# Moving the gating unit's layer norm, the query tiles and the first pair's set-up to other places of a one-core hybrid layer

## The reference, cut to what matters

```python
proj = xn @ p['w_in']
rw, gu, gv, q, gt = jnp.split(proj, [N_SHIFT, N_SHIFT + W, N_SHIFT + 2 * W, N_SHIFT + 3 * W], axis=-1)
rw_s = rw + p['mu_shift'] * (prev - rw)          # prev: the row of the token before
a_out, wkv_new = rwkv7_mix(rw_s, ...)            # 16 heads, matrix state, token recurrence
b_out, v_rows = sgu_mix(gu, gv, ...)             # gelu(gu) * (w_s @ layernorm(gelu(gv)) + b_s)
c_out = mem_xattn(q, mem_k, mem_v)               # 4 heads of 256 over 256 memory rows
gates = jax.nn.sigmoid(gt.reshape(B, T, N_BRANCH, D_MODEL))
mix = jnp.sum(gates * br, axis=2) @ p['w_out']   # br: the three outputs times w_branch
...
y = h + rmsnorm(f, p['g_post_ffn'])              # f: the channel mixer with its convolution
```

## Time and profile before

| | |
|---|---|
| median of 3 runs | 2741.54 us (2741.31 to 2742.99) |
| the profiled execution | 2740.34 us, of which the span from first to last instruction is 2738.4 us |
| PE busy | 2474.8 us, 90% of the span |
| DVE, ACT, POOL busy | 1532.1, 862.1, 98.6 us |
| granted TensorE clock, mean | 0.954 of 2.4 GHz |
| DMA | 346.73 MB, 127 GB/s on average |

### The profile page before, as it was taken

The page is one execution under the profiler, slowest core; times in us unless marked ns, Lnnn a source line. Parts: engine busy times, 40 slices in busy tenths (PEclk is TensorE's granted clock), DMA queues, the critical chain, the costliest instruction groups (busy, mean ns, idle before and its releaser), DMA issues.

```text
span 2738.4 us, 50132 instructions
## 1 busy us (share of the span) xinstructions
PE 2474.8 (90%) x19707; PEld 2321.2 (85%) x19707; DVE 1532.1 (56%) x2207; ACT 862.1 (31%) x940; POOL 98.6 (4%) x171
## 2 busy tenths in 40 slices
PE   5999998996899988988989898699999999999975
PEld 4799977895778777877789897699999999999975
DVE  4533443455556654665554435766566666666665
ACT  4343323422212221222133333333333333323323
POOL 2000000001000000000000000000000000000001
PEclk9999979997999999999999998799999999999987
DMA  5544327632223223322254433144444444444431
GB/s 183 192 145 146 123 92 247 242 108 61 71 78 89 78 89 96 89 73 70 82 155 145 153 124 121 62 154 139 153 138 154 153 143 148 141 155 148 150 126 51
DMA packets 280241, 346.73 MB, mean 127 GB/s; under 512 B 6735, under 2 KB 240511, under 8 KB 278381
## 3 DMA queue, kind: packets, MB, share of 16 engines
q1 hardware_dynamic: 270365, 308.44, 35.2%
q0 software_dynamic: 9712, 36.30, 4.1%
q10 hardware_dynamic: 32, 0.01, 0.0%
HBM read 333.83 MB, written 10.89 MB: 126 GB/s over the span
## 4 chain that ended last, share of the span: by engine, by line
PE 70%; DVE 15%; ACT 6%; issue 6%; DMA 2%; DVEq 1%; POOL 1%; ACTq 0%; SPq 0%; POOLq 0%
PE bank L225 21%; PE bank L227 19%; PE bank L226 19%; PE bank L1030 6%; ACT hi L209 3%; DVE lo L216 3%; DVE rw L1885 2%; DVE work L788 1%; DVE q L712 1%; DMA work<-in_cache_mem_k 1%; PE bank L427 1%; DVE rw L1883 1%; DMA raw<-in_w_branch 1%; PE bank L1450 1%; ACT rw L1827 1%
## 5 line engine op out<-in xcount | busy, mean ns | idle before, releaser
L225 PE MATMUL bank<-ah,hi 128*128 128x320 f32 x3232 | 1040.7, 322 | 50.4 <-DVE lo L216 27.1
L226 PE MATMUL bank<-al,hi 128*128 128x320 f32 x3232 | 1009.4, 312 | 0.0
L227 PE MATMUL bank<-ah,lo 128*128 128x320 f32 x3232 | 1009.4, 312 | 0.0
L216 DVE TENSOR_TENSOR lo<-raw,hi 128x2048 fp32r<-128x2048 f32 x286 | 655.7, 2293 | 626.7 <-ACT hi L209 612.9
L209 ACT ACTIVATE hi<-raw 128x2048 fp32r<-128x2048 f32 x286 | 547.7, 1915 | 1220.1 <-PE bank L227 1183.3
L225 PEld LDWEIGHTS bank<-ah,hi 128*128 128x128 f32 x3232 | 616.7, 191 | 79.4 <-issue 54.7
L226 PEld LDWEIGHTS bank<-al,hi 128*128 128x128 f32 x3232 | 617.9, 191 | 1.8 <-issue 0.4
L227 PEld LDWEIGHTS bank<-ah,lo 128*128 128x128 f32 x3232 | 616.7, 191 | 0.0
L225 PE MATMUL bank<-bh,hi 128*128 128x320 f32 x1088 | 346.2, 318 | 19.1 <-DVE bl L1900 18.3
L226 PE MATMUL bank<-bl,hi 128*128 128x320 f32 x1088 | 336.7, 309 | 0.0
L227 PE MATMUL bank<-bh,lo 128*128 128x320 f32 x1088 | 336.6, 309 | 0.0
(11 more groups left out here) (332 smaller groups left out, 1762.6 us busy)
## 6 DMA issues: line engine op xcount, KB each, us to landing
raw<-in_w_in SPq DMA_DIRECT2D x98, 1024.0 KB, 5.3
raw<-in_w_up SPq DMA_DIRECT2D x88, 1024.0 KB, 5.1
raw<-in_w_down SPq DMA_DIRECT2D x44, 1024.0 KB, 5.0
raw<-in_w_branch SPq DMA_DIRECT2D x24, 1024.0 KB, 5.7
raw<-in_w_out SPq DMA_DIRECT2D x16, 1024.0 KB, 5.4
raw<-in_w_mem_k SPq DMA_DIRECT2D x8, 1024.0 KB, 5.3
raw<-in_w_mem_v SPq DMA_DIRECT2D x8, 1024.0 KB, 5.0
work<-in_cache_mem_k POOLq DMA_DIRECT2D x8, 1024.0 KB, 5.7
```

The lines of the kernel that those rows point to most:

```text
L216: dve.tensor_tensor(lo[c % NS][:, :], raw[c % 2][:, :], hi[c % NS][:, :], ALU.subtract)\
L225: pe.matmul(out, a_hi, b_hi, start=first, stop=False)
L226: pe.matmul(out, a_hi, b_lo, start=False, stop=False)
L227: return pe.matmul(out, a_lo, b_hi, start=False, stop=last)
```

## The change

- The first units are now 16 (`guv_*`): first gv, then gu. The mean of v, its subtraction, the squares and their sum are made inside this stage, beside gu's units. The matmul of the mean stands between the loops over units.
- q's 8 units move behind it. `Beside` gives out 34 units: q's 8, then the rwkv tiles in the order `RW_ORDER` (the tiles of the low-rank inputs first). There are 66 steps before sc0's own (kt0 has 14 of them), 11 per sample as before, 48 in the prompt's pieces, 2 before `wz` and 3 before `wq` (two places in the first pair's set-up), and 65 after.
- In the gating unit the spatial weights are turned before v; four of the gates have 3 steps ahead of them instead of 1.
- ACT evicts an rwkv tile with three instructions instead of two; the samples' first tokens get their old state from one DVE instruction for all tiles.
- Attention's output is split per head of 256 (`split_heads_*`), three of the four inside the prompt's pieces; the low-rank inputs (`low_act`, `sg`) are made there too. Zeroing `mix` moves from DVE to POOL (`mix_zero`), late in attention.
- The first keys go to the place of the values, and are loaded before the gating unit ends. `sgu_parts` is stored behind the second keys and the first values instead of ahead of the first keys.
- The turned last rows (`shift_*`) and their stores move behind the branch stage.

```diff
-        STEPS_RW = {"g0": 4, "g1": 12, "vt0": 9, "vt4": 1, "vt5": 1, "wt0": 1, "wt1": 1, "rep": 2, "gate0": 5, "gate4": 1, "gate5": 1,
-                    "gate6": 1, "gate7": 1, "kt0": 12}
+        UNITS_W, U_W, T_W = 34, U_GUQ + 16, T_GUQ + 16
+        RW_ORDER = (12, 0, 4, 8, 1, 2, 3, 5, 6, 7, 9, 10, 11)
+        STEPS_RW = {"g1": 2, "rep": 8, "vt0": 19, "vt2": 1, "vt4": 2, "vt5": 2, "gate0": 5, "gate2": 1, "gate4": 3, "gate5": 3, "gate6": 3,
+                    "gate7": 3, "kt0": 14, "wz": 2, "wq": 3}
...
+            loop(0, 3)
+            pe.wait_ge(S("v_sum"), 1)
+            pe.matmul(bank[4][:, 0:T], ones[:, :], v_mu, start=True, stop=True).then_inc(S("sgu_ps"), 1)
+            loop(3, 4)
...
+            products(STEPS_RW["wz"])
             pe.wait_ge(S("low_ready"), 1)
             pe.wait_ge(S("pair_in"), 64)
...
+            products(STEPS_RW["wq"])
             pe.wait_ge(S("kk_sq"), 1)
             pe.matmul(pbank("ssq")[:, 0:T], blk[:, :], sq, start=True, stop=True).then_inc(S("wkv_ps"), 1)
+            products(ALL_W)
...
+                if n >= 2 and n % 2 == 0:
+                    split_heads_dve(dve, vv, n // 2 - 1)
+                if n == 5:
+                    dve.wait_ge(S("sig_g"), 3)
+                    vv.do(dve.tensor_scalar(sg, sg, 0.5, 0.5, ALU.mult, ALU.add), "low_ready")
...
+        def split_heads_act(act, aa, h):
+            act.wait_ge(S("at_v"), 3 * NB + 4 * h + 4)
             act.wait_ge(S("sgu_away"), 32)
-            aa.do(act.activation(bh[:, :, :], q[:, :, 0:T], ACT.Copy), "bh_ready")
+            aa.do(act.activation(bh[:, 2 * h:2 * h + 2, :], q[:, 2 * h:2 * h + 2, 0:T], ACT.Copy), "heads_hi")
...
-            vv.do(dve.memset(mixf, 0.0))
...
+            pp.do(pool.memset(mixf, 0.0), "mix_zero")
...
+            keys(0)
+            pool.wait_ge(S("bl_ready"), 1)
+            keys(1)
             values(0)
-            keys(1)
+            for n, src in enumerate((bh, bl)):
+                pool.dma_start(A["sgu_parts"][n], src[:, :, :].rearrange("p k t -> p (k t)")).then_inc(S("sgu_away"), 16)
...
             branch_pe(pe)
+            shift_pe(pe)
             out_pe(pe)
```

More of the change, by code:

```diff
@@ L536, in hybrid_step @@
             STEPS_RW.update({ps_: 2, pp_: 2, po_: 2})
-        ORDER_RW = ["g0", "g1"] + [f"vt{f}" for f in range(6)] + ["wt0", "wt1", "rep"] + [f"gate{g}" for g in range(8)] + ["kt0"]
+        ORDER_RW = ["g1", "rep"] + [f"vt{f}" for f in range(6)] + [f"gate{g}" for g in range(8)] + ["kt0"]
         for names in ATT_B:
@@ L1200, in sgu_dve @@
             vv.do(dve.tensor_scalar(v_rs, bank[5][:, 0:T], 1.0 / W, LN_EPS, ALU.mult, ALU.add), "v_var")
+            for n in range(2):
+                dve.wait_ge(S("sgu_ps"), 3 + n)
+                vv.do(dve.tensor_tensor(ws_t[:, 4 * n:4 * n + 4, :], bank[6 + n][:, :].rearrange("p (g t) -> p g t", g=4),
+                                        bmid(m_u[:, :], 4), ALU.mult), "ws_out")
+            beside.before("rep")
             dve.wait_ge(S("v_std"), 1)
@@ L1241, in sgu_act @@
                                  ACT.Copy), "bs_samples")
+            for f in range(6):
+                beside.before(f"vt{f}")
+                act.wait_ge(S("sgu_ps"), 6 + f)
+                m = TS if f >= 4 else P
+                aa.do(act.activation(vtok[0:m, f // 2, 512 * (f % 2):512 * (f % 2) + 512], bank[4 + f % 4][0:m, :], ACT.Copy), "vt_out")
             beside.before("gate7")
@@ L1256, in products @@
                     next(steps)
-            products("g0")
-            pe.wait_ge(S("v_sum"), 1)
-            end(pe.matmul(bank[4][:, 0:T], ones[:, :], v_mu, start=True, stop=True))
             products("g1")
@@ L1263, in sgu_pe @@
             end(pe.matmul(bank[5][:, 0:T], ones[:, :], v_rs, start=True, stop=True))
+            pe.wait_ge(S("ws_in"), 16)
+            for n in range(2):
+                for k in range(4):
+                    last = pe.transpose(bank[6 + n][:, 128 * k:128 * k + 128], ws_raw[:, 4 * n + k, :], ident[:, :])
+                end(last)
+            products("rep")
+            pe.wait_ge(S("ws_out"), 2)
+            end(pe.matmul(bank[4][0:TS, 0:64], rep8, ws_t[0:8, :, 0:8], start=True, stop=True))
             for f in range(6):
@@ L1272, in sgu_pe @@
                 end(last)
-            pe.wait_ge(S("ws_in"), 16)
-            for n in range(2):
-                products(f"wt{n}")
-                pe.wait_ge(S("vt_out"), 3 + n)
-                for k in range(4):
-                    last = pe.transpose(bank[6 + n][:, 128 * k:128 * k + 128], ws_raw[:, 4 * n + k, :], ident[:, :])
-                end(last)
-            products("rep")
-            pe.wait_ge(S("vt_out"), 6)
-            pe.wait_ge(S("ws_out"), 2)
-            end(pe.matmul(bank[4][0:TS, 0:64], rep8, ws_t[0:8, :, 0:8], start=True, stop=True))
             products("gate0")
@@ L1363, in queries @@
                 vv.do(dve.tensor_copy(qb, q[:, :, TP + 8 * b:TP + 8 * b + 32]), "qb")
+            beside.before("kt0")
+            for t in range(4):
+                dve.wait_ge(S(f"tile_out{t}"), T_RW // 4)
             queries(0)
```

356 lines of the change are left out of this document (192 added, 164 removed).

## The result

The changed kernel takes 2666.54 us (2659.62 to 2669.52, 4 runs), the one before beside it 2742.26 us (2741.31 to 2748.97, 4 runs): a ratio of 0.9715, 95% interval 0.9689 to 0.9741. That is faster by 75.7 us. The prediction was 2683 with a range of 2671 to 2705: right in sign and in its stretch, and 4.5 us outside its range, on the fast side. Two further measurements of the same kernel gave 2668.46 and 2669.18 us, 1.8 to 2.5 us outside.

A forecast was written before the change was run, and what follows sets the result against it. PE was taken as the bound, losing about 76 us to waits and half clock from 317.48 to 655.68. Repriced part by part, the first pair starts at 597.2, not 655.7: gain 58.5, so 2683 us, range 2671 to 2705.

The forecast's parts named there:

- To the gates' start: Gating unit before the gates: 34.3 us of steps plus 4.3 of small matmuls, waits for mean and lo gone, ending at 300.6.
- Layer norm beside gu: Mean and squares made beside gu's units: stretch begins at 261.7, 0.3 us lost after the mean, up to 3 in the range.
- Gates: The gates' small matmuls and 13 steps: 25.2 us at full clock plus 5 lost to some 10 at half clock, to 330.8.
- First keys: Between gates and samples: 12.3 us of steps and 1.7 for keys, the 10.1 us wait gone, to 344.8.
- Samples: The eight attention samples: 116.4 us plus 4 for late DMA loads, bounds 0 and 10, to 465.2.
- Prompt: The prompt's pieces: 61.05 us as before plus 3.5 for new DVE and ACT work, bounds 0 and 10, to 529.8.
- Zeroing on POOL: Zeroing mix late in attention: 4.33 us leave DVE; possible hold-up of 0 to 4.4 us, taken as 0 in the sum.
- Last units and set-up: After attention: 70 steps at 61.6 us, low-rank matmuls 1.4, late hi 0.5, to 593.3; pair's start 3.9 more, to 597.2.
- the second rival: A new wait takes part back (gates at half clock, prompt and weights' loads, or memset): 2688 to 2703, all 2720; chance 0.22.
- 2 us for each of 34 units: Rival of a late ACT and DVE feed stopping PE at every unit: 2751 at 2 us each, slower than before; chance 0.03.
- out stage: Transposes and evictions ahead of mix's rounding cost 0; stores of the last rows, 10 us before DVE asks, cost 0 too.
- rival 3: Better than summed: clock holds in the gates, no new wait, pair's start at full clock: 2670 to 2673; chance 0.11.

The follow-up runs named there:

- r4: Changed kernel with the 13 steps among the gates spread evenly (two ahead of six gates, one ahead of the last): 2662.99 us, ratio 0.9717.
- r12: Changed kernel with evenly spread gate steps and the two reads of the gating unit's parts inside pair 5: 2665.43 us, ratio 0.9719.
- r8: Changed kernel with both head splits' first keys issued behind the stores of the gating unit's parts: 2679.48 us, ratio 0.9768.
- r11: Changed kernel with the zeroing of mix back on DVE, behind the pair's preparation: 2669.17 us, ratio 0.9741.
- r7: Changed kernel with 64 of the 65 covering steps put ahead of the first pair's set-up: 2679.36 us, ratio 0.9774.
- r13: Changed kernel with the residual's loads ahead of the turned rows' stores again, run beside the unchanged one on the same chip: 2674.57 us, ratio 0.975.
- r14: Changed kernel, unedited, run again on the same chip as the version with the residual's loads moved back: 2669.18 us, ratio 0.9733.
- r3: Kernel before, with the residual's loads held until the branch stage's last unit but one is done: 2735.97 us, ratio 0.9975.
- r2: Changed kernel with the residual's loads back at the branch stage's start, ahead of the last rows' stores: 2668.77 us, ratio 0.9729.
- r1: Changed kernel, unedited, run once more as a yardstick: 2668.46 us, ratio 0.9726.
- r9: Kernel before, with the two reads of the gating unit's parts issued inside pair 5, behind the pair's state: 2736.25 us, ratio 0.9982.
- r10: Changed kernel with the two reads of the gating unit's parts issued inside pair 5: 2668.0 us, ratio 0.973.
- r5: Kernel before, with 22 more words in `rw` so that the buffers behind it begin on multiples of 64 bytes: 2741.61 us, ratio 1.0001.
- r6: Changed kernel with `keep_mu` allocated ahead, so that the buffers no longer begin on multiples of 64 bytes: 2662.53 us, ratio 0.9712.

## Why the prediction was off

By its own steps, on the profiled execution:

- *To the gates' start*: 300.6 predicted, 301.1 measured. Layer norm beside gu and the feed's arithmetic were right: no wait for mean or lo.
- *Gates*: 330.8 predicted, 332.0 measured. Half clock for 10.2 us where "some 10" was said, in the gates that have one step among them. r4 and r12 show that the spacing of the steps decides whether there is any. That the length came out so closely is luck: in other runs with the same steps it is 3.4 or 13.7 us.
- *First keys*: the point that answers to 344.8, the end of the first keys' transposes, lies at 346.3: 14.4 us behind the gates where 14.0 were said, the rest being the 1.2 us that were late already. The window of this stage ends 2 steps later, with the first scores at 348.3; the sum had these two steps in the samples' 1.9. The wait went (10.1 to 0.9) and r8 brought 6.8 back.
- *Samples*: 465.2 predicted, 464.9 measured; from the first scores they took 116.7 us where the sum had 118.5. The transfers that I priced at 4 us cost 0.9, a wait for the keys behind them, and none for weights. Yet a unit's weights landed later than anywhere else in these two traces. Their hi began at 365.87, at once behind the landing, and no wait of PE for a lo followed. The one issue of SP from 347 to 349 us, after:

```profile
raw<-in_w_in SPq DMA_DIRECT2D x1, 1024.0 KB, 18.7
```

  The price rested on a slack of 9.8 us for a load, from two units of 7.04 us. That is the pace of units without work beside them. By the earlier trace rows a sample gives out 11 steps in 14.29 us, so a unit of 8 steps takes some 10.4 us there and the same working leaves a load about 16.5 us, and more slack behind it (estimates from these rows). In a window of one sample's length (364.0 to 378.3 us) the DMA engines were busy 0.91 of the time (0.80 in the earlier trace rows).
- *Prompt*: to 529.8 predicted, 527.9 measured; 63.0 us and not 64.5, so 1.9 us above where 3.5 was said.
- *Zeroing on POOL*: cost 0, as taken. The trace after has the two engines together:

```profile
518.96 4.37 POOL L683 MEMSET mix<- 128x5120 f32 x1 [6.47 <-PE bank L1510]
```
```profile
522.21 0.15 DVE L1390 TENSOR_SCALAR rw<-rw 128x1 f32<-128x1 f32 x1
...
523.04 0.42 DVE L1440 COPY q<-bank 128x256 f32<-128x256 f32 x1 [0.67 <-PE bank L1581]
...
524.36 0.16 DVE L1394 RECIPROCAL rw<-rw 128x1 f32<-128x1 f32 x1
524.56 0.35 DVE L1395 TENSOR_SCALAR small<-small,rw 128x256 f32<-128x256 f32 x1
```

  Inside the memset (518.96 to 523.33) a scaling took 0.15 us and a copy 0.42, their usual lengths. The long scaling began 1.2 us after the memset's end, so the Trainium skill's rule of contention ("SBUF — State Buffer", section "Who interferes with whom") was not put to the test on such an instruction. The meeting cost nothing here. r11 shows what it costs to have the zeroing on DVE ahead of the logarithms: 6.8 us in this stretch, where I had only "4.33 us leave DVE".
- *Last units and set-up*: first pair's start 596.4 (597.2 less the first two matmuls' 0.74), measured 595.1. r7 shows the cover's worth: 12.7 us of wait.

The stretch as a whole was thus off by 1.3 us, which is closer than its terms were: 1.6 us too little up to the first scores and 0.7 in the last units stand against 1.8 us too much for the samples and 1.6 for the prompt. Three slips in the prediction's rivals change nothing: 2683 less 9 to 13 is 2670 to 2674, the second rival begins at 2687 and not at 2688, and 2 us for each of 34 units are 68 and not 59, which added to 2683 gives the same 2751.

The step that failed is the last sentence of the out stage: "The stores of the last rows ... cost 0 too", and with it the silence on what is queued behind them. I had priced the stores alone. Behind them on GpSimd's queue stand the residual's loads, though, and by going late with the stores these loads leave the way free for a unit's weights. The term that stood at 0 is a gain: 7.1 us in the profile, 5.4 (r13 against r14) and 6.9 us (r3) in the medians, and 0.3 in the pair with the fewest executions (r2 against r1, four each). Every instruction behind a moved wait moves too, and I had not listed them. It could be read from the trace of before: a hi waits 13.06 us for its weights, with 3.2 MB issued just ahead of them.

The second omission is in the pairs, which the sum took as unchanged; they became 7.2 us shorter. The full clock at the first pair's start, 2.7 us, stood only in rival 3, though the sum had PE busy right up to it; the sum should have had it. And pair 5 became 6.0 us shorter in these profiles. r9 shows what a meeting costs there in the kernel before (4.4 us) and r10 that the kernel after has nothing left to gain. Why the reads land faster after the change is open. They are issued at the same distance from their neighbours. Whether buffers begin on multiples of 64 bytes is excluded as the cause (r5, r6). r8 differs from the kernel after in the order of keys and stores alone and has 94.6 us, and r13, whose edit lies behind the pairs, has 93.1. So the length of pair 5 does not follow from the code in it alone.

Together 7.2 and 7.1 us, less 3.5 that other stages gave back, are 10.8 us; with the stretch's 1.3 that makes 12.1 of the 12.3 us between 2681.8 and the profiled 2669.5. Between 2683 and the median of 2666.5 there are 16.5 us; the other 4.2 are how far the two profiled executions lie from their medians (1.2 below before, 3.0 above after), which is chance. Rival 3 had named a time of 2670 to 2673, for the gates' clock, which did not hold in the kernel after, for no new wait, and for the pair's start at full clock, which did come. The result lies below that too.

## What to carry to other kernels

When a wait moves on a queue, list what stands behind it and ask of each transfer not only who will want it sooner, but whom it was delaying: a load issued long before its use can cost more than one issued late. In an engine that feeds the weights in program order, look for the longest wait of the split for a transfer, and at what was issued on all queues just ahead of it. Price such a meeting with the pace that the units have at that place, not with their fastest. Spread the covering steps evenly among small matmuls: here two steps ahead of each gate kept the full clock (r4, r12), and a run of four gates with one step among them had 3.4 to 13.7 us of half clock.

## What the runs showed of the hardware

Executions of the same kernel spread over some 10 us (2659.62 to 2669.52), far more than I had thought from the three runs of before. The mean granted clock goes with it: 0.966 and 0.965 in the two slowest of the four, 0.970 in the fastest. In which stage these executions differ is not shown, as only one of them was profiled; the three profiles of this kernel have loops of 635.5 to 637.3 us. How far the clock can move a stage is seen across the runs, whose pairs have the same instructions but for the place of two reads in r10. Windows from the first pair to the eighth of the kernel after and of r10:

```profile
595.15:1232.45 637.30, 572.88 (x6828) 499.00 (x6827) 387.54 (x671) 154.46 (x155) 37.41 (x66) 0.97 0.27 82
```
```profile
594.90:1224.00 629.10, 564.55 (x6827) 491.57 (x6826) 387.29 (x671) 154.47 (x155) 37.33 (x66) 0.99 0.27 83
```

DVE, ACT and POOL are busy for the same time to within 0.3 us; PE's busy time follows the granted clock, 572.88 us at 0.97 and 564.55 at 0.99. r6 and r11 lie between, with 632.5 and 631.3 us. So a single profile with a loop that is 5 us shorter proves nothing for an edit elsewhere; the stage that was edited must show it. r2 and r11 are cases where one median hid a stage's 5 to 7 us.

The second surprise was that neither load on the DMA engines nor a late landing costs anything by itself. In the samples after the change the engines are busy 0.75 of the time, a unit's weights take 18.7 us to land, and PE waits for no weights. In the branch stage 14.8 us cost 5.0 us of PE's time and half clock behind it, and in pair 5 16.4 us cost 3.3, while 13.3 us there cost no such wait. In all of these a megabyte or more was issued on GpSimd's queue within a few us of the weights. As far as these rows show, the slack at the place decided the cost: units follow each other every 7.04 us in the branch stage and about every 10.4 us in the samples (estimated above), and in the pairs ACT has the pair's own instructions queued behind the hi that waits. In r8 the price was a wait of 6.8 us for the keys, not for weights.
